# The early mean of the HGRN2 mixers' output rows taken a row later, and the scores' first level as a product with the identity

## The reference, cut to what matters

```python
for l in range(DEPTH_2):
    x = layer_norm(ALPHA * x + 0.5 * swiglu_2(x, ffn1_gate[l], ...), ln_g[l, 0], ln_b[l, 0])   # stage a0, a1
    h = x @ w_in[l]                                                                          # stage h0, h1
    u = h[..., :D_POOL]
    q, f_raw, v, g = jnp.split(h[..., D_POOL:], 4, axis=-1)
    y_pool = multiscale_pool(u, pool_w[l], pool_scale[l])
    o = hgrn2_recurrence(q, f_raw, v, lb_all[l])
    y_hgrn = head_rms_norm(o, hgrn_norm_g[l]) * jax.nn.silu(g)
    mix = jnp.concatenate([y_pool, y_hgrn], axis=-1) @ w_out[l]
    x = layer_norm(ALPHA * x + mix, ln_g[l, 1], ln_b[l, 1])
    x = layer_norm(ALPHA * x + 0.5 * swiglu_2(x, ffn2_gate[l], ...), ln_g[l, 2], ln_b[l, 2])   # stage b0, b1
```

## Time and profile before

| | |
|---|---|
| median of three runs | 3010.27 us |
| the profiled execution | 3008.45 us |
| its span, first to last instruction | 3006.7 us |
| TensorE busy with matmuls | 2938.9 us, 98% |
| VectorE, ScalarE, GpSimd busy | 44%, 33%, 13% |
| granted clock of TensorE, mean | 0.992 |
| HBM | 86 GB/s over the span |

### The profile page before, as it was taken

How to read it: one execution, slowest core, us unless ns; L and a number is a source line. 1 busy time by engine, 2 the same in 40 slices (tenths; PEclk the granted TensorE clock), 3 DMA queues, 4 the chain that set the end, 5 groups by cost and what they waited for, 6 DMA issues and landing times.

```text
span 3006.7 us, 32392 instructions
## 1 busy us (share of the span) xinstructions
PE 2938.9 (98%) x13550; PEld 2419.8 (80%) x13550; DVE 1326.0 (44%) x1783; ACT 1004.1 (33%) x1345; POOL 405.4 (13%) x426
## 2 busy tenths in 40 slices
PE   9999989999999999999999999999999999899998
PEld 7888877577888888888887888888888788788887
DVE  5453267654342333334656333343333465543324
ACT  4232234453232233223334332233322332342222
POOL 3110056411110000011231000100001113200010
PEclk9999999999999999999999999999999999999999
DMA  4223312122333233222212233223323221232232
GB/s 143 94 97 98 98 52 68 24 77 84 98 98 97 85 99 98 96 94 84 78 49 70 91 98 98 91 84 98 97 94 97 77 73 55 64 98 95 95 98 77
DMA packets 76017, 260.40 MB, mean 87 GB/s; under 512 B 11728, under 2 KB 11856, under 8 KB 75856
## 3 DMA queue, kind: packets, MB, share of 16 engines
q1 hardware_dynamic: 75872, 258.34, 26.9%
HBM read 255.03 MB, written 2.10 MB: 86 GB/s over the span
## 4 chain that ended last, share of the span: by engine, by line
PE 91%; DVE 6%; ACT 1%; issue 1%; SPq 0%; POOL 0%; DMA 0%; DVEq 0%; ACTq 0%; POOLq 0%
PE bank L325 25%; PE bank L326 25%; PE bank L327 25%; PE bank L341 2%; PE bank L347 2%; PE bank L342 2%; PE bank L691 2%; PE bank L444 1%; PE bank L455 1%; DVE Hl L1301 1%; PE bank L381 1%; PE bank L377 1%; PE bank L378 1%; PE bank L436 1%; DVE Hl L1299 1%
## 5 line engine op out<-in xcount | busy, mean ns | idle before, releaser
L1293 DVE TENSOR_TENSOR wlo<-wraw,whi 128x1024 fp32r<-128x1024 f32 x474 | 587.5, 1252 | 822.5 <-ACT whi L802 822.0
L325 PE MATMUL bank<-Hh,whi 128*128 128x512 f32 x2320 | 910.4, 392 | 19.4 <-DVE wlo L1293 14.7
L327 PE MATMUL bank<-Hl,whi 128*128 128x512 f32 x2320 | 905.2, 390 | 0.0
L326 PE MATMUL bank<-Hh,wlo 128*128 128x512 f32 x2320 | 905.0, 390 | 0.0
L802 ACT ACTIVATE whi<-wraw 128x1024 fp32r<-128x1024 f32 x479 | 499.8, 1057 | 943.3 <-DMA wraw<-weights 942.9
L325 PEld LDWEIGHTS bank<-Hh,whi 128*128 128x128 f32 x2320 | 437.0, 188 | 117.0 <-issue 21.3
L327 PEld LDWEIGHTS bank<-Hl,whi 128*128 128x128 f32 x2320 | 436.8, 188 | 91.7
L326 PEld LDWEIGHTS bank<-Hh,wlo 128*128 128x128 f32 x2320 | 437.0, 188 | 88.8
L325 PE MATMUL bank<-Ah,whi 128*128 128x512 f32 x1056 | 411.8, 390 | 0.0
L327 PE MATMUL bank<-Al,whi 128*128 128x512 f32 x1056 | 410.9, 389 | 0.0
L326 PE MATMUL bank<-Ah,wlo 128*128 128x512 f32 x1056 | 410.8, 389 | 0.0
(11 more groups left out here) (259 smaller groups left out, 2548.9 us busy)
## 6 DMA issues: line engine op xcount, KB each, us to landing
wraw<-weights SPq DMA_DIRECT2D x479, 512.0 KB, 3.5
X<-x_t SPq DMA_DIRECT2D x8, 256.0 KB, 6.8
y_t<-X SPq DMA_DIRECT2D x8, 256.0 KB, 2.0
Y<-masks SPq DMA_DIRECT2D x1, 512.0 KB, 9.1
MUb<-ssm SPq DMA_DIRECT2D x1, 256.0 KB, 8.3
tmp<-ssm SPq DMA_DIRECT2D x1, 256.0 KB, 3.8
zsum<-attention SPq DMA_DIRECT2D x1, 256.0 KB, 3.8
MUb<-attention SPq DMA_DIRECT2D x1, 256.0 KB, 4.2
```

Source lines behind the costliest of these rows:

```text
L325: pe.matmul(b, sh, mh, start=start, stop=False)
L326: pe.matmul(b, sl, mh, start=False, stop=False)
L327: signal(pe.matmul(b, sh, ml, start=False, stop=stop), keys)
L1293: dve.tensor_tensor(wlo[:, u % NS, :], wraw[:, u % NS, :], f32(whi[:, u % NS, :]), SUB).then_inc(*S.done("weights_lo", ("lo", u)))
```

## The change

Three things. In the mixers' output rows (nk == KD, `late`), the centre's column sums are taken in row 3 behind its first tile, the spread behind row 3's last tile, and everything that needs the early mean, the copy to MUb, GpSimd's shifts, the subtractions and the first squares, comes with row 4. Which rows make the early mean, and the FFN stages, stay. Level 0 of the scores is written by a product of the bank with the identity, in place of a masked copy. And the memset of `Sc`, with GpSimd's wait ahead of it and the waits for it on ScalarE and VectorE, is gone.

```diff
@@ -500,8 +500,9 @@
 
...
             for nb in rows(ln_mid(st, nk)):
-                if nb == 3:
-                    for k in range(4):
+                late = nk == KD
+                if nb == 3 + late:
+                    for k in range(4 + late):
                         bank_squares(st, k)
...
                     bank_squares(st, nb)
@@ -517,11 +518,11 @@
 
...
             def mid(k, nb):
-                if nb == 2 and k == nk // 2:
+                if (nb, k) == ((2, nk // 2) if nk > KD else (3, 4)):
                     b = open_bank((st, "centre"))
...
                     col_sums(zsum[:, :], b, True, (("full", (st, "centre")),))
-                if nb == 3 and k == nk // 2 + 1:
+                if (nb, k) == ((3, nk // 2 + 1) if nk > KD else (3, 7)):
                     spread(0, (st, "mu"), ("spread", (st, "mu")))
...
                     for name, src, ready in (("sum z", zsum, ("z", st, 6)), ("sum zz", acc, ("acc", st))):
@@ -923,9 +924,11 @@
                     split_hi(then, k, X[:, k, :])
...
         def out_ln(st, nk, ends, then, li, acc_free, used):
+            late = nk == KD
             for nb in range(KD):
-                if nb == 3:
-                    hi_to(ends[nb] - nk + nk // 2 + 1)
+                if nb == 3 + late:
+                    if not late:
+                        hi_to(ends[nb] - nk + nk // 2 + 1)
                     act.wait_ge(*S.at(("full", (st, "mu"))))
...
                         act.wait_ge(*S.at(used))
@@ -934,14 +937,14 @@
                 hi_to(ends[nb] - 1)
...
                     table(ACT.Sqrt)
-                if nb == 3:
+                if nb == 3 + late:
                     act.wait_ge(*S.at(("Y centred", st, 0)))
...
                         square(st, k, Y[:, k, :])
-                elif nb > 3:
+                if nb > 3:
                     act.wait_ge(*S.at(("Y", st, nb)))
...
                         square(st, nb, Y[:, nb, :])
@@ -1172,8 +1175,6 @@
                     *S.done("rows_out", ("U3", st, g), empties=[((st, "u"), g)]))
...
             def far(n):
-                if n == P:
-                    act.wait_ge(*S.at(("scores zero", st)))
                 for h in range(4):
...
                     b = bank(use)
@@ -1402,9 +1403,10 @@
             rest(KD - 1)
...
         def out_ln(st, nk, ends, then, xs, half, y_free, last):
+            late = nk == KD
             for nb in range(KD):
-                if nb == 2:
-                    lo_to(ends[nb] - nk + nk // 2)
+                if nb == 2 + late:
+                    lo_to(ends[nb] - 1 if late else ends[nb] - nk + nk // 2)
                     dve.wait_ge(*S.at(("full", (st, "centre"))))
...
                     dve.tensor_scalar(rcol[:, 16:20], b[:, 0:4 * WIDE:WIDE], 1.0 / 256, None, MUL).then_inc(
@@ -1412,7 +1414,8 @@
                     dve.tensor_scalar(rcol[:, 20:24], b[:, 0:4 * WIDE:WIDE], 1.0 / 512, None, MUL).then_inc(
...
                 if nb == 3:
-                    lo_to(ends[nb] - nk + nk // 2 + 1)
+                    if not late:
+                        lo_to(ends[nb] - nk + nk // 2 + 1)
                     dve.wait_ge(*S.at(("mean col", st)))
...
                 lo_to(ends[nb] - 1)
@@ -1435,7 +1438,7 @@
                             *S.done("rows", ("Y centred", st, k)))
...
                             add_square(st, k, st)
-                elif nb > 3 and nb < KD - 1:
+                if 3 < nb < KD - 1:
                     add_square(st, nb, st)
...
             dve.wait_ge(*S.at(("full", (st, "sum z"))))
@@ -1883,10 +1886,12 @@
                     mk = msk[:, li, :].unsqueeze(1).to_broadcast([P, 4, P])
...
                     dve.wait_ge(*S.at(("full", use)))
-                    if li:
-                        dve.wait_ge(*S.at(("Sc", st, li - 1, h)))
-                    elif h == 0:
-                        dve.wait_ge(*S.at(("scores zero", st)))
+                    if not li:
+                        dve.tensor_tensor(view, src, ident.unsqueeze(1).to_broadcast([P, 4, P]), MUL).then_inc(
+                            *S.done("decays", ("Sc", st, li, h), empties=[use]))
+                        continue
+                    dve.wait_ge(*S.at(("Sc", st, li - 1, h)))
+                    if h == 0:
                         dve.wait_ge(*S.at("masks kept"))
...
                 decays(li + 1)
@@ -2037,7 +2042,7 @@
             pool.wait_ge(*S.at(zsum_free))
...
             for nb in range(2, 7):
-                if nb == 3:
+                if nb == (3 if st != xs + "o" else 4):
                     pool.wait_ge(*S.at(("mu", st)))
...
                     for k in range(4, KD):
@@ -2122,8 +2127,6 @@
                 pool.wait_ge(*S.at(("state", j)))
...
         def mixer_2(st, a):
-            pool.wait_ge(*S.at(("full", (a, "row", 7))))
-            pool.memset(Sc[:, :, :, :], 0.0).then_inc(*S.done("pool_rows", ("scores zero", st)))
             pool.wait_ge(*S.at(("X", a, KD - 1)))
...
```

## The result

The changed kernel takes 2990.11 us (median of four runs, 2988.90 to 2990.41), against 3010.22 us for the kernel before beside it: 20.1 us less, a ratio of 0.9932 with a 95% interval of 0.992 to 0.9943. The forecast was 2992.7 us with a range of 2987.0 to 2997.5. The profiled execution took 2988.90 us around a span of 2987.1, 19.6 us less than the span before.

A forecast was written before the change was run, and what follows sets the result against it. TensorE, busy 98% of the span, bounds the kernel, so gains come only where it stands still. Memset 6.9, second mixer 6.8 and first mixer 3.9 make 17.6 us: 3010.27 - 17.6 = 2992.7 us, range 2987.0 to 2997.5.

The forecast's parts named there:

- The memset: Ahead of the second mixer, removing it frees VectorE's small copy and TensorE's restart: 6.9 us gained; 0 ahead of the first.
- The product: Level 0 of the scores: eight identity products replace masked copies, hidden behind VectorE's waits for TensorE; taken at 0.
- The rival on the slow side: Products ahead of each mixer's first decay cost 3 us more each, making the kernel slower than before; chance 0.03.
- Waits 1 to 3: Mixers' rows: centre waits (2.45, 1.60 us) go, spread waits (0.88, 1.99) go, row 4's shifted X is hidden.
- Wait 4: Mixers' rows: GpSimd's shifts and add of Y[4] delay VectorE's first two subtractions by 1.1 + 1.3 us.
- Step 5: VectorE and ScalarE chain, first subtraction to row 7's sums: 14.3 us; gains 6.8 us second mixer, 3.9 first.
- The sum: Whole kernel: 6.9 + 6.8 + 3.9 = 17.6 us saved, giving 2992.7 us; chance 0.52.
- rival (b): Slow restart of 1.5 us behind second mixer's new waits, plus collisions up to 2 us; gain 12.6 to 16.1; chance 0.2.
- Rival (a): Mixers' rows: no collision of VectorE and GpSimd, chain ends ahead of TensorE; gain 22.6 us, 2987.7 us; chance 0.2.

The follow-up runs named there:

- run 2: Kernel before with only the memset and its waits taken away and level 0 as a product: 3003.70 us, ratio 0.9978.
- run 3: Kernel before with its memset kept whole but waiting for X[0] of the stage before, so running behind the small copies: 3003.42 us, ratio 0.9978.
- Run 1: Changed kernel with the memset, its waits and the masked copies put back, so only the mean a row later: 2996.48 us, ratio 0.9956.
- run 4: Kernel before with row 4's weight unit moved ahead of the subtractions and squares in the mixers' rows: 3006.55 us, ratio 0.9989.
- run 5: Changed kernel with GpSimd's add of Y[4] into zsum only behind VectorE's second subtraction in the mixers' rows: 2987.14 us, ratio 0.9918.
- run 8: Changed kernel with the add of Y[4] behind the second subtraction and the shifts of X[6] and X[7] behind the fourth: 2986.46 us, ratio 0.9921.
- run 6: Changed kernel with column sums behind row 7's last tile and four filler matmuls left out, in all six layer norms: 2982.09 us, ratio 0.9901.
- run 9: Kernel before with its memset cut into four pieces, one per head, at the same place: 3006.67 us, ratio 0.9986.

## Why the prediction was right, step by step

- **The memset.** 6.9 us predicted from the two transitions; 6.9 in the trace, 6.6 and 6.9 in runs 2 and 3. The cause is shown: with the memset moved the gain is the same, and with it cut up the copy's wait is cut up. The two parts, 4.6 us for the copy and 2.3 for TensorE's slow restart, are in the trace too: each profile with a copy of 4.8 us (the kernel before, runs 1 and 4) has the lower clock behind it and a transition of 30.2 us, and none of the others has. That it costs nothing ahead of h0 holds too: nothing there moved by more than 0.05 us in run 2.
- **The product.** Taken at 0, and 0.04 us less each in the trace. The rival on the slow side, a product that costs 3 us more, is out.
- **Waits 1 to 3.** Those for the centre and the spread are gone in both mixers, and row 4 does not wait for its shifted X, as worked out.
- **Wait 4**, the collisions. I took 1.1 + 1.3 us, 2.4 in each mixer; they cost 2.06 in h1 and 2.03 in h0. Runs 5 and 8 take them apart in h0: 1.1 us for the add and 0.9 for the last shift. So both were somewhat smaller than I took them. I counted a GpSimd operation from the end of the subtraction, but the add of Y[4] only held the second subtraction for the rest of its length.
- **Step 5**, the chain of squares. The waits in row 7 were to be 0.9 and 0.5 us in h1, and 1.8 in h0; they are 0.58, 0.41 and 1.45. The gains were 7.3 for 6.8, and 4.3 for 3.9 us.
- **The sum.** 17.6 us predicted and 18.5 found in the three places. The 19.6 us between the two spans hold 1.1 us that come from elsewhere, mostly from stretches of slow clock in one execution and not in another, and the medians, 20.1 us apart, will hold some of the kind. The prediction had no term for that: it took them as standing where they stood. Its rival (b), a slow restart in h1 behind the new waits, did not come; behind the 1.45 us in h0 it did, as it had behind 1.22 us before: in the changed kernel the clock is 0.83 over 1622 to 1632 us, with the slow part behind the sums. Run 1, with a wait of 1.21 us at the same place, has none there.

```profile
1622.00:1632.00 10.00, 8.55 (x49) 7.49 (x47) 4.58 (x10) 3.76 (x6) 1.27 (x1) 0.83 0.18 54
```

- **Rival (a)**, no collisions, would have been 2987.7 us. The median of 2990.11 is 2.4 us from it and 2.6 from the forecast, so the total does not choose between them. The traces rule it out: the collisions are in the rows, and taking them away made the kernel faster. A slip of no weight: the range was to take in (b) whole, and (b) reaches to 2997.7, 0.2 us above it.

## What to carry to other kernels

Work on GpSimd that nobody waits for can still hold up the kernel, if a small SBUF copy of VectorE on the critical path begins beside it: here the copy stood for what was left of the memset, 4.65 us, and TensorE lost 2.3 us more at a lower clock behind the stop. Look for tiny VectorE operations with long durations. Moving the GpSimd operation can do as much as removing it; run 3 had the whole gain by one changed wait.

When work is moved later to end a wait, write down what it now runs beside: here 2 us of VectorE's time in each set of rows went to GpSimd operations that had met nothing of the kind before. And where an engine holds filler work ahead of a wait, first see whether real work from ahead of the fillers can take their place, as the column sums did in run 6 for 1.0 to 1.1 us in each layer norm of an FFN stage.

## What was not expected of the hardware

- A memset of 6.96 us beside full-width VectorE operations with two SBUF inputs cost them nothing (0.69 us each, run 3), while GpSimd additions beside the same kind of operation cost up to 1.1 us a meeting (runs 5 and 8). In the kernel before, the first showed only in that nothing was late ahead of h0.
- One small operation with one SBUF input was held off by a memset, the copy, and another was not, the reciprocal (0.18 us, run 9). What sets them apart no run shows.
- The same stop of TensorE is followed by a slow stretch in one execution and not in another: 0.83 and 1.00 of the clock from 680 to 690 us in two kernels that are alike up to there. That is 1.6 us for one stretch: ahead of it the changed kernel is 1.3 us later than the kernel before, and behind it 0.2 us earlier.
